# A first RMS norm split over two stages of a fused two-block kernel: squares on ScalarE and sums on GpSimd during the first modulation, scaling and shift at the head of the query projection

## The reference, cut to what matters

```python
mod = silu(c) @ w_ada + b_ada             # also for c_ctx; sh1, sc1 are its first two parts
h   = rmsnorm(x,   norm_mix_w) * (1 + sc1)  + sh1      # 1024 latent positions
hc  = rmsnorm(ctx, norm_mix_w) * (1 + csc1) + csh1     # 256 context positions
p, pc = h @ w_in, hc @ w_in[:, :CTX_COLS]              # query, key, value, recurrence, gates
...
lower_bounds = cumsum(softmax(hgrn_lb_logits, axis=1), axis=1)     # used much later
...
h = sin(freq0 * (feats @ w1 + b1)); h = sin(freq1 * (h @ w2 + b2)); h = (h @ w3) * window
filters = h * rsqrt(sum(h * h) + eps)                  # block 2's filters, from weights alone
```

## Time and profile before

| | us |
|---|---|
| median of 3 runs | 4048.88 |
| the three runs | 4029.77, 4054.28, 4048.88 |
| the profiled execution, its own time | 4044.17 |
| its span in the profile | 4042.5 |
| mean granted TensorE clock, share of full | 0.92 |

### The profile page before, as it was taken

How to read it: one execution, slowest core, us unless ns; L and a number is a source line. 1 busy time by engine, 2 the same in 40 slices (tenths; PEclk the granted TensorE clock), 3 DMA queues, 4 the chain that set the end, 5 groups by cost and what they waited for, 6 DMA issues and landing times. The chain is left out here.

```text
span 4042.5 us, 39915 instructions
## 1 busy us (share of the span) xinstructions
PE 3619.5 (90%) x15730; PEld 2735.9 (68%) x15730; DVE 1753.4 (43%) x3007; ACT 1001.1 (25%) x1623; POOL 110.0 (3%) x187
## 2 busy tenths in 40 slices
PE   7769999988879998999999798898878789999997
PEld 4336566655568876888888586676456668888886
DVE  5324440444532335353444754345575343334345
ACT  1334421122223213111111323253120231111112
POOL 0000000000001000000000000101000000000000
PEclk8888889698869999999999899999879889999998
DMA  5300021000013322222222213304323211111111
GB/s 206 140 26 1 1 99 35 11 11 21 1 55 133 104 84 89 93 83 73 83 83 73 91 43 91 103 24 135 97 94 126 72 52 42 52 52 42 52 52 42
DMA packets 75773, 279.54 MB, mean 69 GB/s; under 512 B 10583, under 2 KB 30039, under 8 KB 58104
## 3 DMA queue, kind: packets, MB, share of 16 engines
q1 hardware_dynamic: 37048, 166.63, 12.1%
q0 software_dynamic: 21936, 102.66, 7.0%
q10 hardware_dynamic: 16656, 8.42, 1.2%
HBM read 246.11 MB, written 31.59 MB: 69 GB/s over the span
## 5 line engine op out<-in xcount | busy, mean ns | idle before, releaser
L1815 PE MATMUL banks<-input_parts,weight_parts 128*128 128x512 f32 x1408 | 549.7, 390 | 32.7 <-DVE weight_parts L1876 32.7
L1816 PE MATMUL banks<-input_parts,weight_parts 128*128 128x512 f32 x1408 | 549.0, 390 | 0.0
L1817 PE MATMUL banks<-input_parts,weight_parts 128*128 128x512 f32 x1408 | 548.9, 390 | 0.0
L1815 PEld LDWEIGHTS banks<-input_parts,weight_parts 128*128 128x128 f32 x1408 | 265.2, 188 | 90.2 <-DVE weight_parts L1876 35.1
L1889 DVE TENSOR_TENSOR before_split<-before_split,banks 128x512 f32<-128x512 f32 x88 | 60.5, 688 | 575.2 <-PE banks L1817 575.2
L1898 DVE SCALAR_TENSOR_TENSOR x<-banks,parameters,x 128x512 f32<-128x512 f32 x352 | 254.8, 748 | 113.7 <-PE banks L1817 113.2
L1816 PEld LDWEIGHTS banks<-input_parts,weight_parts 128*128 128x128 f32 x1408 | 265.3, 188 | 55.2
L1817 PEld LDWEIGHTS banks<-input_parts,weight_parts 128*128 128x128 f32 x1408 | 265.0, 188 | 55.2
L1815 PE MATMUL banks<-hidden_parts,weight_parts 128*128 128x512 f32 x704 | 273.9, 389 | 0.0
L1816 PE MATMUL banks<-hidden_parts,weight_parts 128*128 128x512 f32 x704 | 273.9, 389 | 0.0
L1817 PE MATMUL banks<-hidden_parts,weight_parts 128*128 128x512 f32 x704 | 273.9, 389 | 0.0
(11 more groups left out here) (494 smaller groups left out, 5936.3 us busy)
## 6 DMA issues: line engine op xcount, KB each, us to landing
weight_ring<-in_w_gu SPq DMA_DIRECT2D x44, 1024.0 KB, 4.8
weight_ring<-in_mod_w POOLq DMA_DIRECT2D x24, 1024.0 KB, 5.3
weight_ring<-in_w_down SPq DMA_DIRECT2D x22, 1024.0 KB, 4.8
weight_ring<-in_w_merge SPq DMA_DIRECT2D x24, 512.0 KB, 3.6
weight_ring<-in_dft SPq DMA_DIRECT2D x12, 1024.0 KB, 5.0
x<-in_x_t POOLq DMA_DIRECT2D x2, 4096.0 KB, 17.9
weight_ring<-in_w_ada_rest POOLq DMA_DIRECT2D x8, 1024.0 KB, 5.3
work<-in_w_ada_rest POOLq DMA_DIRECT2D x8, 1024.0 KB, 5.3
```

Source lines behind the costliest of these rows:

```text
L1815: e.matmul(bank, w_hi, hi, start=(k == 0), stop=False)
L1816: e.matmul(bank, w_hi, lo, start=False, stop=False)
L1817: mm = e.matmul(bank, w_lo, hi, start=False, stop=(k == len(terms) - 1))
```

## The change

The stages `bounds` and `norm_mix` go, and their work is spread:

- **Squares and sums.** A new class `InputSquares` squares the 24 tiles on ScalarE, three behind each filter square of `modulation_1` (the `yield 3` in the filter network's scalar part), in the order first half, second half, context. The first tile's square of each span goes straight into the sum, the other 21 go through two buffers, and GpSimd adds them to the sum, one `tensor_tensor` each. ScalarE waits for an add before it writes a buffer again.
- **Sum over partitions and roots.** TensorE needs three products with ones in place of 24 (512, 512 and 256 wide), ahead of the last filter sum. ScalarE takes three Ln and three Exp between its last square and the filters' Sqrt.
- **Scaling and shift.** They stand at the head of `attention_q` on VectorE and ScalarE, latents first. The query projection is written out by hand, in the order (tile 0, half 0), (tile 1, half 0), (tile 0, half 1), (tile 1, half 1), and waits for the shifted tiles one by one.
- **The bounds.** Differences and Exp stand at the start of `modulation_1`, quotients at its end. `sc_mix` follows the scales directly.
- **The filters' reciprocal** moves behind the modulation work beside `attention_q`. The buffer SUM of the filter network takes the place of `e2`, and the second weight buffer of `modulation_rest` moves in memory.

```diff
@@ filter_network
+            if c == NCH:
+                e.wait_ge(f_cp, NCH)
+                xs.tensor(e)
...
             e.activation(scr[:, c % 2, :], HT[:, c % 2, :], ACT.Square).then_inc(sq_rd.sem, 1)
+            yield 3
+        xs.roots(e)
         ss_rd.wait(e, NCH)
         e.activation(rn, pg.ps[:, 6:8, 0:256], ACT.Sqrt, bias=pg.eps[:, 0:1]).then_inc(rt_rd.sem, 1)
...
+    def vector_after(e):
         rt_rd.wait(e, 1)
-        ch(e.reciprocal(rn, rn))
+        pg.vchain(e)(e.reciprocal(rn, rn))
+    pg.filter_after = vector_after
@@ class InputSquares
+    def scalar(e):
+        e.wait_ge(self.pg.x_loaded, 32)
+        for i, (s, k, v) in enumerate(self.tiles):
+            a = self.adds_below(i)
+            if k and a >= 2:
+                e.wait_ge(self.added, a - 1)
+            dst = self.buf[a % 2][:, 0:v.shape[-1]] if k else self.sums[s]
+            e.activation(dst, v, ACT.Square).then_inc(self.squared, 1)
+            yield
+    def pool(self, e):
+        for i, (s, k, v) in enumerate(self.tiles):
+            a = self.adds_below(i)
+            if k:
+                e.wait_ge(self.squared, i + 1)
+                if a:
+                    e.wait_ge(self.added, a)
+                e.tensor_tensor(self.sums[s], self.sums[s], self.buf[a % 2][:, 0:v.shape[-1]], ALU.add).then_inc(self.added, 1)
+    def tensor(self, e):
+        e.wait_ge(self.added, 3 * (KT - 1))
+        e.wait_ge(self.squared, 3 * KT)
+        for s in range(2):
+            e.matmul(self.pg.ps[:, 4 + s, :], self.pg.ones, self.sums[s], start=True, stop=True).then_inc(self.summed, 1)
+        e.wait_ge(self.logs, 1)
+        e.matmul(self.pg.ps[:, 4, 0:TC], self.pg.ones, self.sums[2], start=True, stop=True).then_inc(self.summed, 1)
+    def roots(self, e):
+        for s in range(3):
+            e.wait_ge(self.summed, s + 1)
+            w = self.rs[s].shape[-1]
+            e.activation(self.rs[s], self.pg.ps[:, 4 + s % 2, 0:w], ACT.Ln, bias=self.pg.eps[:, 0:1], scale=1.0 / D).then_inc(self.logs, 1)
+        e.wait_ge(self.logs, 3)
+        for s in range(3):
+            e.activation(self.rs[s], self.rs[s], ACT.Exp, scale=-0.5)
@@ window_attention, attention_q
+                for k in range(KT):
+                    if g == 0 and t == 0:
+                        n_ready.wait(e, KT * s + k + 1)
+                    mm = e.matmul(...)
...
+    def q_scalar(e):
+        for s, (_, dst, j) in enumerate(spans):
+            for k in range(KT):
+                n_scaled.wait(e, KT * s + k + 1)
+                e.activation(dst[:, k, :], dst[:, k, :], ACT.Identity, bias=pg.mod1[:, k, j:j + 1]).then_inc(n_ready.sem, 1)
+        beside[1](e)
...
+    def q_vector(e):
+        for s, (src, dst, j) in enumerate(spans):
+            for k in range(KT):
+                e.scalar_tensor_tensor(out=dst[:, k, :], in0=src[:, k, :], scalar=pg.sc_mix[:, k, j:j + 1],
+                                       in1=pg.input_squares.rs[s], op0=ALU.mult, op1=ALU.mult).then_inc(n_scaled.sem, 1)
...
-    pg.stages[-1].update(gpsimd=beside[0], vector=beside[2], scalar=in_turn(beside[1], pg.stages[-1]["scalar"]))
+    pg.stages[-1].update(gpsimd=beside[0], scalar=q_scalar, vector=in_turn(q_vector, beside[2], pg.filter_after))
```

More of the change, by code:

```diff
@@ new lines, with __init__, adds_below, scalar @@
+class InputSquares:
+    def __init__(self, pg):
+        self.pg = pg
+        x, ctx = pg.x, pg.ctx_raw
+        self.tiles = [(s, k, x[:, k, s * HALF:(s + 1) * HALF]) for s in range(2) for k in range(KT)] + [(2, k, ctx[:, k, :]) for k in range(KT)]
+        m = Mem(pg.big, M_ROOTS, M_END - 4 * D)
+        rs, buf = m(TA), m(HALF)
+        self.rs = [rs[:, 0:HALF], rs[:, HALF:T], rs[:, T:TA]]
+        self.sums = [pg.spare[:, 0, 0:HALF], pg.spare[:, 0, HALF:T], pg.spare[:, 1, 0:TC]]
+        self.buf = [buf, pg.spare[:, 1, TC:TC + HALF]]
+        self.squared, self.added = pg.sem("input_squares"), pg.sem("input_squares_added")
+        self.summed, self.logs = pg.sem("input_sums"), pg.sem("input_logs")
+    def adds_below(self, i):
+        return i - -(-i // KT)
+    def scalar(self, e):
+        e.wait_ge(self.pg.x_loaded, 32)
[29 more added lines that the diff above has]
+            e.activation(self.rs[s], self.rs[s], ACT.Exp, scale=-0.5)
@@ L809, in scalar @@
         yield
+        yield from xs.scalar(e)
+    lb_terms, lb_bounds, lb_exps = bounds(pg)
+    pg.input_squares = xs = InputSquares(pg)
     def vector(e):
@@ L923, in setup, with bounds @@
     modulation_first(pg)
+def bounds(pg):
     pg.lb = pg.perm_left(8)
@@ L935, in scalar2, with differences @@
         e.activation(ea, ea, ACT.Exp).then_inc(lb_exp, 1)
-    def vector2(e):
+    def differences(e):
         ch = pg.vchain(e)
-        for j in range(2):
-            e.scalar_tensor_tensor(out=pg.sc_mix[:, :, j], in0=pg.mod1[:, 8:16, j], scalar=1.0,
-                                   in1=pg.param("norm_mix"), op0=ALU.add, op1=ALU.mult)
         lb = pg.param("lb")
@@ L958, in vector2 @@
         ch(e.tensor_tensor(pg.one_minus_lb, ea, mx, ALU.mult))
[L960 to L971 removed]
+    return differences, quotients, exps
 LAT = [(TC, TC + HALF), (TC + HALF, TA)]
@@ new lines, in window_attention, with q_sync, q_tensor @@
+    f0 = pg.fill
+    g0 = pg.take_groups([f0 + 4, f0 + 8])
+    pg.fill += 8
+    def q_sync(e):
+        for g in range(2):
+            pg.load(e, g0 + g, pg.d["w_q"][g])
+    def q_tensor(e):
+        for g in range(2):
+            slot = pg.weights(e, g0 + g)
+            for n, (t, s) in enumerate(order):
+                f = f0 + 4 * g + n
+                pg.bank_free(e, f)
+                a, b = LAT[s]
+                for k in range(KT):
+                    if g == 0 and t == 0:
+                        n_ready.wait(e, KT * s + k + 1)
+                    mm = e.matmul(pg.ps[:, f % 8, :], slot[:, (2 * k + t) * P:(2 * k + t + 1) * P], h1[:, k, a:b],
+                                  start=(k == 0), stop=(k == KT - 1))
+                mm.then_inc(pg.ps_full, 1)
@@ new lines, in q_scalar @@
+    def q_scalar(e):
[4 more added lines that the diff above has]
+        beside[1](e)
+        e.wait_ge(pg.ps_free, f0)
+        for g in range(2):
+            for n, (t, s) in enumerate(order):
+                f = f0 + 4 * g + n
+                e.wait_ge(pg.ps_full, f + 1)
+                e.activation(q[:, 2 * g + t, s * HALF:(s + 1) * HALF], pg.ps[:, f % 8, :], ACT.Copy).then_inc(pg.ps_free, 1)
```

45 lines of the change are left out of this document (23 added, 22 removed).

## The result

The changed kernel takes 3994.79 us (median of 7 runs, 3990.34 to 4019.27), the kernel before, run again beside it, 4036.66 us (7 runs, 4029.77 to 4054.28). The ratio is 0.9901, with a 95% interval of 0.9872 to 0.9931: faster by 1.0%, 41.9 us. I had forecast 4013.3 in a range of 3998 to 4026, so the time lies 3.2 us under the range. The profiled execution took 3992.39 us (span 3990.7).

A forecast was written before the change was run, and what follows sets the result against it. TensorE's feed-forward products make most of the bounding chain, but the norm leaves TensorE idle. Starting the query projection 38.0 us earlier, less 2.4 of contention, gives 35.6 us (0.88%): 4048.88 to 4013.3 us, range 3998 to 4026.

The forecast's parts named there:

- The path: From the last modulation product to the first query projection product: 38.0 us shorter, 35.6 after 2.4 of contention.
- Sums: Three TensorE products for 24 after the last modulation product: 4.73 us at the low clock.
- Last filter sum: L710 on TensorE beside the roots: 3.50 us, covered.
- Roots: ScalarE's last Ln, table load, three Exp, table load and Sqrt after the sums, ending at 106.76.
- Tail contention: End of modulation_1: VectorE's reductions delay GpSimd's last three adds; 2.4 us taken, bounds 0 and 5.5.
- Middle: Middle of modulation_1: adds delay VectorE at most 3.5 us against 3.96 of slack; nothing taken, upper bound 6.7 us.
- adds over 2 us: Sign of being wrong: GpSimd's adds in modulation_1 taking over 2 us, where 1.1 to 1.2 were expected.
- Cover in the projection: Scaling and shift run beside the query projection; VectorE done at about 157, projection at 166, covered with 9 us.
- The kinder clock (1): No tail contention, and a higher TensorE clock in sums and projection: gain at most 43.0 us, 4006; chance 0.25.
- GpSimd held back (2): Adds wait for VectorE's train, or VectorE is late mid-stage: gain 32.5 down to 25.8 us, 4016 to 4023; chance 0.21.
- Lockstep (3): ScalarE, GpSimd and VectorE wait on each other in modulation_1: 47 us against the 38.0, 4058; chance 0.03.
- against the median 4048.88 - 35.6 = 4013.3: Final step: the gain of 35.6 us subtracted from the median of three runs of the kernel before.

The follow-up runs named there:

- e2: The changed kernel run again with no edit; 3991.04 us (5 runs), ratio 0.9886 to the kernel before.
- e4: The changed kernel without GpSimd's 21 adds, so with another result; 3994.18 us (1 run).
- e1: The kernel before, run again with no edit for a second profile; 4036.45 us (1 run).
- e5: The kernel before with the bounds alone moved to the start and end of modulation_1; 4029.65 us (10 runs), ratio 0.9987.
- e8: The kernel before with each of GpSimd's eight products in block 2 waiting for the one ahead; 4032.67 us (10 runs), ratio 0.9994.
- e12: The kernel before, run again with no edit for a third profile; 4040.58 us (1 run).

## Why the prediction was wrong

**The path** was right, nearly term by term. The gain at the first projection product was forecast at 35.6 us and is 35.7. That the product starts where it was forecast (110.63 for 110.8) is in part luck, since e2 starts it at 106.00; the gain over the stretch, 35.5 to 37.4, is what repeats.

- *Sums.* Their start was forecast at 99.0 and is 98.97. They take until 103.4 instead of 103.7, with the clock low at first, as supposed.
- *Last filter sum.* It took 1.94 us, not 3.50; it is covered, so it was worth nothing.
- *Roots.* Forecast 106.76 after sums at 96.63, thus 10.1 us; it took 9.9, from 98.97 to the end of the Sqrt at 108.85.
- *Start of the projection.* 1.8 us behind the Sqrt, 1.6 forecast.
- *Tail contention.* 2.4 forecast; TensorE stood 2.42 in this profile and 1.88 in e2, and e4 makes it 1.6 to 2.6. The mechanism, one reduction's turn ahead of each add, is what the rows show. That an add takes 1.52 us in such turns and a reduction 1.73 is the part that I had not priced.
- *Middle.* Nothing forecast, nothing found: TensorE was busy for all 59.56 us. Yet a 512-wide add took 2.06 us there and a reduction 2.28, and "adds over 2 us" was one of the signs of being wrong that I had set. The sign was a bad one, since VectorE's slack took the turns: after three of them the window product was over at 72.32, 0.83 us ahead of the L708 that needs it. The slack of 3.96 was near the 4.7 that e4 shows at this place.
- *Cover in the projection.* 13 us forecast by the terms for scaling and shift, 13.0 and 12.6 measured. VectorE was done at 161.7 (157 forecast), the projection at 167.3 (166 forecast), so the cover was 5.6 us and not 9.
- *The adds.* 1.26 and 0.72 us alone, 1.15 and 0.61 assumed.

**Rivals.** The kinder clock (1) is not the cause: the head of the projection had 0.71 in place of 0.51, which is worth 1.1 us in its 5.3, but e2 doesn't repeat it: from the first product of the query projection to the first of `attention_v` (L450, L451 after) it is 76.6 us in e1, 75.6 after and 76.9 in e2. GpSimd held back (2) is refuted: the engines take turns. By the rule of the Trainium skill (SBUF — State Buffer, section "Who interferes with whom"), the one that comes second waits for the whole instruction. The traces agree for one instruction: an add of 0.72 us alone takes 1.52 beside reductions. But an engine with several queued doesn't keep the other out: in the changed kernel GpSimd gets in between any two reductions. Only the eight products of block 2 show a lockout, in the six profiles without an earlier operation on GpSimd or waits between the products. Lockstep (3) is refuted by the middle that didn't move.

**What failed is the step "against the median 4048.88 - 35.6 = 4013.3"**, and the range around it. By the 25 runs beside e5 to e8 the kernel before has a median of 4037.06 and reaches from 4028.02 to 4055.34; the three runs that I had happened to lie with two in the upper part of that, and their median 12 us too high. That was bad luck too: of the 59 other runs of that kernel 5 lie at 4048.88 or above. From the median beside the result the same gain gives 4036.66 - 35.6 = 4001.1, 6.3 us above the measured time. The profile was no better witness: 11.6 of its 4044.17 us were a low clock in the recurrence. I had noted that it lay 4.7 us below the median and taken the difference for scatter of the execution, not as a sign that the base itself was open by that much. The range took in one term of downward scatter, some 8 us, where one of the three runs lay 19 us below.

**A term was missing**: 3.6 us in block 2, in a place that I had read the earlier trace rows for the price of the contention, without asking whether the change could reach it.

Together: 4036.66 - 35.7 - 3.6 = 3997.4 against 3994.79 measured. The other 2.6 us are within what medians of 7 runs tell. By all 12 runs of the changed kernel (median 3993.6, lowest 3990.34) and the 25 of the kernel before (4037.06, 4028.02), the gain is 43.5 by the medians and 37.7 by the lowest, with 39.3 named. In the column of the rest it is 3887.8 before (the mean of e1 and e12) and 3881.6 after (after and e2), 6.2 less, 3.6 of it found. What the other few us are, if they are anything, stays open: the rest is 3880.1 to 3887.0 in the six profiles with adds, and 3886.4 and 3889.2 for one program in e12 and e1, without a cause in the code.

## What to carry to other kernels

Work that stands alone between two stages of a matmul-bound kernel is worth its whole length once it is moved beneath them, and the sum over one path, row by row, gave that length here to within 2 us (35.6 for 35.5 to 37.4). Such a sum is a difference and not a time: when few runs are known, take the base and the range from how far apart the runs and the stages of the profile lie. Adds on GpSimd beside VectorE are free only while VectorE has slack for turns of both; count the adds that can meet one VectorE train, and spread them. Before the starts of one place in two profiles are compared, look whether the clock ran alike ahead of it.

## What the hardware showed that I had not expected

- GpSimd and VectorE, both with instructions queued on SBUF, alternate: a 512-wide add 2.06 us (1.26 alone) and a reduction 2.28 (1.22 alone); a 256-wide add 1.52 (0.72 alone) with a reduction of 1.73. A pair comes every 2.2 us (1.66 with the 256-wide add), somewhat less than the sum of the two alone, 2.48 (1.94).
- The same two engines can also lock out: eight 256-wide products back to back (4.62 us) let a waiting 0.41 us multiply end only after 4.29, in all six profiles in which the products had no wait between them and no tensor operation of GpSimd ahead of them. A tiny GpSimd operation early in the program turned this into turns, and so did a wait between the products.
- Executions of one program differ by the granted clock in single places: 90.3 or 78.7 us for one part of the recurrence, and the last modulation product of `modulation_1` anywhere from 96.0 to 102.3.
